# First layer of a two-layer trunk: where on TensorE a group of w_ada's sums is turned into columns

## The reference, cut to what matters

```
def adaln_params(cvec, w_ada, b_ada):
    m = jax.nn.silu(cvec) @ w_ada + b_ada
    return jnp.split(m, 6, axis=-1)
...
sh1, sc1, gt1, sh2, sc2, gt2 = [m[:, None, :] for m in adaln_params(c, w_ada, b_ada)]
shc1, scc1, gtc1, shc2, scc2, gtc2 = adaln_params(c_ctx, w_ada, b_ada)
...
x = x + gt1 * (mix @ w_out)
x = x + gt2 * conv_ffn(modulate(rmsnorm(x, g2), sh2, sc2), w_up, ffn_conv, w_down)
```

## Time and profile before

| | |
|---|---|
| median of three runs | 2159.57 us (2153.75 to 2161.0) |
| profiled execution | 2152.7 us, of which the span from first to last instruction is 2150.9 us |
| TensorE matmul busy | 2085.3 us, 97% |
| VectorE, ScalarE, GpSimd busy | 1432.5, 1086.7 and 486.6 us |
| mean granted TensorE clock | 0.984 |
| first layer's feed-forward network | from about 271 to 654 us of the span |

### The profile page before, as it was taken

How to read it: one execution, slowest core, us unless ns; L and a number is a source line. 1 busy time by engine, 2 the same in 40 slices (tenths; PEclk the granted TensorE clock), 3 DMA queues, 4 the chain that set the end, 5 groups by cost and what they waited for, 6 DMA issues and landing times.

```text
span 2150.9 us, 42650 instructions
## 1 busy us (share of the span) xinstructions
PE 2085.3 (97%) x18062; PEld 1981.3 (92%) x18062; DVE 1432.5 (67%) x2724; ACT 1086.7 (51%) x1881; POOL 486.6 (23%) x230
## 2 busy tenths in 40 slices
PE   7999999999999999999889999999999999999999
PEld 5977999999998789999778899999999999999999
DVE  4445378787785667666663666589388897666666
ACT  5333253232235456446433455555677776555564
POOL 1201100000012120002211441288766662000000
PEclk9999999999998999999999999999999999999999
DMA  7345255466663355764221245565544445555664
GB/s 274 111 138 186 86 180 177 161 225 242 217 231 121 124 180 168 246 197 140 79 79 60 69 138 171 170 190 191 170 145 144 148 147 177 195 188 196 196 193 151
DMA packets 97854, 354.90 MB, mean 165 GB/s; under 512 B 10752, under 2 KB 11776, under 8 KB 97408
## 3 DMA queue, kind: packets, MB, share of 16 engines
q1 hardware_dynamic: 97664, 352.18, 49.0%
HBM read 351.09 MB, written 1.05 MB: 164 GB/s over the span
## 4 chain that ended last, share of the span: by engine, by line
PE 87%; DVE 4%; issue 4%; ACT 2%; DMA 2%; POOL 2%; SPq 0%; POOLq 0%; ACTq 0%; DVEq 0%
PE ps L79 82%; PE ps L84 3%; PE ps L106 1%; POOL TL L113 1%; DVE TL L113 1%; DMA RAW<-in_wada 1%; ACT SQ L154 1%; ACT TH L157 1%; DMA AW<-in_wada 0%; DMA RAW<-in_wdn 0%; ACT Hh L157 0%; POOL SM L113 0%; POOL ACC L113 0%; DVE SQ L113 0%; DVE ps L113 0%
## 5 line engine op out<-in xcount | busy, mean ns | idle before, releaser
L157 ACT ACTIVATE TH<-RAW 128x1024 fp32r<-128x1024 f32 (+1 forms) x515 | 539.7, 1049 | 282.5 <-PE ps L79 255.9
L113 DVE TENSOR_TENSOR TL<-RAW,TH 128x1024 fp32r<-128x1024 f32 (+1 forms) x339 | 417.4, 1231 | 237.0 <-ACT TH L157 236.7
L113 POOL TENSOR_TENSOR TL<-RAW,TH 128x1024 fp32r<-128x1024 f32 x176 | 423.6, 2409 | 492.1 <-ACT TH L157 462.9
L79 PE MATMUL ps<-Hh,TL 128*128 128x256 f32 x1920 | 448.4, 286 | 9.4 <-DVE TL L113 4.3
L79 PE MATMUL ps<-Hl,TH 128*128 128x256 f32 x1920 | 437.0, 280 | 0.4 <-DVE Hl L113 0.4
L79 PE MATMUL ps<-Hh,TH 128*128 128x256 f32 x1920 | 437.0, 280 | 0.0
L79 PE MATMUL ps<-HXh,TL 128*128 128x256 f32 x1314 | 365.8, 283 | 4.3 <-POOL TL L113 2.5
L79 PE MATMUL ps<-HXh,TH 128*128 128x256 f32 x1314 | 360.9, 279 | 0.0
L79 PE MATMUL ps<-HXl,TH 128*128 128x256 f32 x1314 | 360.1, 278 | 0.0
L79 PEld LDWEIGHTS ps<-Hh,TL 128*128 128x128 f32 x1920 | 319.7, 190 | 35.3 <-issue 19.4
L79 PEld LDWEIGHTS ps<-Hh,TH 128*128 128x128 f32 x1920 | 320.1, 190 | 0.7 <-issue 0.5
(11 more groups left out here) (338 smaller groups left out, 3113.3 us busy)
## 6 DMA issues: line engine op xcount, KB each, us to landing
RAW<-in_ut SPq DMA_DIRECT2D x128, 512.0 KB, 3.3
RAW<-in_v SPq DMA_DIRECT2D x128, 512.0 KB, 3.4
RAW<-in_wup SPq DMA_DIRECT2D x88, 512.0 KB, 4.3
AV<-in_wada SPq DMA_DIRECT2D x80, 512.0 KB, 3.8
RAW<-in_win SPq DMA_DIRECT2D x74, 512.0 KB, 3.6
RAW<-in_wada SPq DMA_DIRECT2D x56, 512.0 KB, 3.8
RAW<-in_wdn SPq DMA_DIRECT2D x32, 512.0 KB, 4.3
RAW<-in_wout SPq DMA_DIRECT2D x24, 512.0 KB, 3.7
```

The costliest lines, as they stand in the source:

```text
L79: return self.e.matmul(out, lhs, rhs, start=first, stop=last, skip_group_check=skip)
L113: return DRY if self.e is None else self.e.tensor_tensor(out, a, b, op)
L157: return DRY if self.e is None else self.e.activation(out, a, ACT.Copy, **kw)
```

## The change

The places of `columns` of groups 11 to 28 and of group 9 move. Nothing is added or removed, and no DMA moves.

```diff
 def ada_steps(g, i):
-    return g - 1 if g - 1 in ADA_ADDED and i % 4 == 1 else None, g - 1 if i % 4 == 3 else None
+    if g == ADA_ADDED[0]:
+        return None, g - 1 if i % 4 == 3 else None
+    return g - 1 if i % 4 == 1 else None, g - 2 if i % 4 == 1 and g - 2 in ADA_ADDED else None
...
                     summed, turned = ada_steps(g, i)
+                    if turned:
+                        columns(turned)
                     if summed:
                         ada_sums(summed)
-                    if turned:
-                        columns(turned)
...
             if l:
+                columns(ADA_ADDED[-2])
                 norm(("n1", l), 512)
...
+            def turn_and_spread():
+                if l == 0:
+                    columns(9)
+                head_spread(1)
...
-                         ks=MIX_ORDER, midway=lambda n: head_spread(1) if n == 4 else None)
-            if l == 0:
-                columns(9)
+                         ks=MIX_ORDER, midway=lambda n: turn_and_spread() if n == 4 else None)
...
-                if i % 4 == 0 and g - 1 in ADA_ADDED:
+                if i % 4 == (0 if g == ADA_ADDED[0] + 1 else 2) and g - 1 in ADA_ADDED and g - 1 < ADA_ADDED[-1]:
                     columns(g - 2)
...
             if l:
+                columns(ADA_ADDED[-2])
                 above(("n1", l), ROOT[0][:, 0:4], 1024 * EPS, "n2", l - 1)
```

## The result

The changed kernel takes 2150.88 us (median of 10 runs, 2143.3 to 2152.43), the kernel before on the same chips 2156.08 (10 runs, 2151.78 to 2161.0). The ratio is 0.997, 95% interval 0.9956 to 0.9983: 0.3% faster, small but clear of no change. The forecast was 2157.7 us, with 0.88 for a change within 0.3%, too small to be told from none. It started from the median of three runs, 2159.57 us; over ten runs the kernel before has 2156.08.

The account below looks back on a forecast made before the run. The prediction took TensorE's own stream to bound the kernel. Gains of 1.8 us (groups 11 to 28) and 0.1 (group 9), with other engines at 0, made 1.9 us off 2159.57: 2157.7 us, range 2150.5 to 2162.

Parts of the forecast that it names:

- What bounds the kernel: First layer's feed-forward network: TensorE is busy 122.00 of 122.00 us and waits for nobody, so only its own stream counts.
- The turn ahead of the sums at 0.12: Groups 11 to 28: a turn directly ahead of a group's sums costs 0.12 us, gaining 0.10 each.
- no gain: Rival: passages into and out of placed products cost, turns cost their own time anywhere; time 2159.6 us, chance 0.14.
- hidden: Rival: the whole turn hides in the passage from fp32r to placed products; gain 4.2 us, time 2155.4, chance 0.10.
- The turn by itself at 0.22: Network's fp32r stream: a lone turn costs 0.22 us, 0.14 for itself and 0.08 on the first pair behind.
- term of 1.8 us: Groups 11 to 28 in the network: 18 moved turns gain 0.10 us each, 1.8 us in all.
- nothing in the sum hangs on the execution: Whole sum: the 1.9 us gain holds for any execution, so it is taken from the runs' median, 2159.57 us.
- The term of the turn of group 9: Turn moved ahead of the head norm's spread: costs 0.12 us instead of 0.22, a gain of 0.10.
- Other engines at 0: ScalarE's copy, VectorE's moved turn steps and SP's DMA requests: the change costs nothing there, 0 us.
- The clock: Rival: the granted clock falls from 2.4 to 1.2 GHz behind turn and sums; time about 2185 us, chance 0.04.
- VectorE late: Rival: VectorE's turn delays a weight tile's low part and TensorE waits; 3.6 us, time 2161.3, chance 0.06.
- How the numbers follow: Closing step: chances are 0.07 faster, 0.88 within 0.3% (6.5 us), 0.05 slower; range from bounds widened by scatter.

## Why the prediction was wrong

*What bounds the kernel*: right. TensorE waits for nobody in the network after either, and what each edit does to its stream came out in the stretch, in the sums above to about 0.1 us.

*The turn ahead of the sums at 0.12*: right. The sums start 0.45 behind the pair (444.56 - 444.11), and the row that priced it came from the second layer. The rival "no gain" needed 0.54 and the rival "hidden" 0.32; both fall. With them falls the rule of TensorEngine Tiling (the Trainium skill, section Key Properties) as the whole of the cost: the passages into placed products did stay as many as they were, and the gain came.

*The turn by itself at 0.22*: this step failed. The prediction says: "Two pairs without it take 2 x 0.235 = 0.47 (the starts around are 0.23 and 0.24 apart)." The 0.22 holds for the turn and the first pair behind it, as the turns done twice and three times show. But the count ended two pairs behind the turn, while its effect goes on to the next fp32 work; the rest was put at nothing without a reason. Two starts could not show it: at two decimals a pair of 0.236 us and one of 0.227 both read 0.23 or 0.24. And the turn of rows 4, that of group 15, is one of three in this network that went the other way, from slow to fast. With one row more of the tile ahead, and the earlier trace rows for the end of the stretch behind the turn:

```profile
426.73 0.40 PE L79 MATMUL ps<-Hh,TH 128*128 128x256 f32 x2
...
431.91 0.40 PE L79 MATMUL ps<-Hl,TH 128*128 128x256 f32 x2
```

Ahead of it 44 matmuls take 431.91 - 426.73 = 5.18 us, 117.7 ns each; behind it 92 take 443.04 - 432.60 = 10.44, 113.5 each. So this turn, read over the whole stretch of 96 matmuls behind it, costs less than nothing (0.22 less 96 x 4.4 ns); one turn was not enough to price eighteen. Of the turns of groups 16 to 27 all twelve went from fast to slow, with 744 matmuls behind them. With this tail such a turn costs 0.22 + 62 x 4.4 ns = 0.49 us, and moving it gains 0.37 instead of 0.10. Over all the moved turns that makes the term of 1.8 us into 4.9 to 5.9, by the pitch with which the execution entered the network, so the sentence that nothing in the sum hangs on the execution fails as well. The term of the turn of group 9 goes from 0.1 to 1.4, since 288 matmuls hung behind it.

*Other engines at 0*: right, shown by VectorE's steps alone.

*The clock, VectorE late*: neither came. The granted clock is 1.00 from 408 to 530 us, and no weight tile was waited for. The 0.2 us for VectorE in rows 3, taken as a sign that it was once close, is the idle time of 0.22 us that the weight load shows behind every group's sums; it was put down to VectorE there.

*How the numbers follow*: the size of the sum put 0.88 on a change too small to be told. The 6 to 7 us are about at the bound of 6.5 that the prediction drew, and ten runs of each told them. The measured 2150.88 lies 6.8 us under the forecast, and 3.5 of these come from the kernel before: its median of three runs was that much above its median of ten. The measured time is at the very edge of the range, whose low end came from scatter and from no mechanism; that it lies inside is luck. (The 0.04 of the clock and the 0.02 of scatter add up to 0.06 for slower, where the prediction has 0.05.)

## What to carry to other kernels

Price an interruption of a matmul stream by the length of a whole stretch behind it and ahead of it, and over several such places, not by the next two starts of one: 4 ns on each of 62 matmuls were more than everything that the local view showed. Where two starts around an event differ by one unit of the last digit, take the distance over 40 of them before calling it rounding; a busy share of 100% hides it. Collecting small fp32 work into one interruption paid here, but which collection it was decided the pitch, so the stretch behind each candidate has to be measured.

## What the runs showed of the hardware that I had not expected

At a granted clock of 1.00 the same fp32r matmuls (128x128 by 128x256) run at one of two steady distances, 113.3 or 117.7 ns, and keep it until other work comes. Counts of what followed which interruption in the first layer, from 215 to 655 us, over all thirteen profiles (the pitch of the last 40 matmuls ahead, and of 40 behind from the fifth on, both at full clock):

| interruption | behind fast | behind slow |
|---|---|---|
| one turn | slow 54 of 54 | fast 10 of 10 |
| two turns | slow 16 of 16 | slow 4 of 4 |
| three turns | slow 17 of 17 | fast 3 of 3 |
| 8 placed | fast 31 of 31 | fast 79 of 79 |
| 16 placed | fast 21 of 21 | slow 17, fast 6 |
| turn, 8 placed | fast 74 of 74 | fast 2 of 2 |
| turn, 4 placed | fast 20 of 20 | none seen |
| turn, 16 placed | slow 25 of 25 | fast 7 of 7 |
| 8 placed, turn | fast 14 of 14 | none seen |
| 16 placed, turn | fast 1, slow 1 | fast 2 of 2 |
| 8 placed, turn, 8 placed | fast 5 of 5 | none seen |

The counts in the expectations were taken from fewer profiles, and their one exception behind a single turn (8 of 9) is not found here. By the starts around these places, less as many fp32r distances at the pitches ahead and behind, a turn by itself costs 0.22 to 0.25 us, 8 placed products 0.54 to 0.55, 16 cost 0.74 to 0.77, and a turn ahead of either adds 0.10 to 0.12.

What lies beneath stays open. A switch at every turn doesn't fit two turns, and a reset by the passage into placed products doesn't fit sixteen. The weight loads of the slow stretches show no idle time either. The table does not hold everywhere: in the second layer a turn with 16 placed products behind it, near 926 us in the kernel before, left the stream fast in all 13 profiles, 9 times behind fast and 4 behind slow. There TensorE had waited 0.2 us for VectorE one matmul ahead. The pitch at the start of the network, behind a DMA wait, differed from execution to execution of the same code, and the groups with 16 sums carried that difference on until the first group with 8.
